# One column chunk of an output projection by seven half products, with another order of the jobs and loads around it

## The reference

```python
out = merge_heads(o_a, o_b, o_c) @ lp["w_o"]
xp = xp + g1 * mix
xp = xp + g2 * hier_moe(modulate(rms_norm(xp, lp["g_ffn"]), sh2, sc2), lp)
# in hier_moe: group logits and expert logits from h, top-1 group, top-2 experts in it, then
return (jax.nn.silu(xblk @ w1[e]) * (xblk @ w3[e])) @ w2[e]
```

## Time and profile before

| | |
|---|---|
| median of three runs | 1645.39 us (1644.51 to 1646.77) |
| the profiled execution | 1645.26 us, its span 1643.1 us |
| TensorE busy | 1532.1 us (93%) |
| weight loads of TensorE | 672.4 us (41%) |
| VectorE busy | 810.6 us (49%) |
| ScalarE, GpSimd busy | 281.4 us (17%), 101.3 us (6%) |
| the chain that ended last | TensorE 56%, DMA 29% of the span |
| matmuls of the projection (L1242) | 170.3 us, 384 records |

### The profile page before, as it was taken

How to read it: one execution, slowest core, us unless ns; L and a number is a source line. 1 busy time by engine, 2 the same in 40 slices (tenths; PEclk the granted TensorE clock), 3 DMA queues, 4 the chain that set the end, 5 groups by cost and what they waited for, 6 DMA issues and landing times.

```text
span 1643.1 us, 18272 instructions
## 1 busy us (share of the span) xinstructions
PE 1532.1 (93%) x6604; PEld 672.4 (41%) x6635; DVE 810.6 (49%) x1471; ACT 281.4 (17%) x746; POOL 101.3 (6%) x185
## 2 busy tenths in 40 slices
PE   6999999999999999999989889989989988988998
PEld 3446655454434444633333333333333333333332
DVE  3783555762365973525434434434434444434444
ACT  3124222122231000110210111111011012011010
POOL 1013100000131001000000000000000000000000
PEclk9999999999999999999999999999999999999999
DMA  9993521667597783999999999999999999999997
GB/s 391 418 413 150 198 110 73 251 247 307 182 391 314 307 326 135 329 399 407 428 428 428 429 428 427 429 427 426 425 428 426 426 427 425 426 428 425 424 424 285
DMA packets 62128, 581.96 MB, mean 354 GB/s; under 512 B 9218, under 2 KB 10178, under 8 KB 16940
## 3 DMA queue, kind: packets, MB, share of 16 engines
q1 hardware_dynamic: 54848, 557.34, 82.1%
q0 software_dynamic: 5936, 23.23, 3.6%
q10 hardware_dynamic: 1296, 0.77, 0.2%
HBM read 584.07 MB, written 7.05 MB: 360 GB/s over the span
## 4 chain that ended last, share of the span: by engine, by line
PE 56%; DMA 29%; DVE 2%; ACT 1%; issue 1%; SPq 1%; POOL 0%; DVEq 0%; ACTq 0%; POOLq 0%
DMA ring<-in_w 29%; PE bank L1539 13%; PE bank L1266 11%; PE bank L1242 9%; PE bank L1570 5%; PE bank L1437 5%; PE bank L1357 2%; PE bank L1488 2%; PE bank L1131 1%; PE bank L1332 1%; PE bank L1589 1%; DVE r L2112 1%; PE bank L1513 1%; PE bank L1340 1%; PE bank L1228 1%
## 5 line engine op out<-in xcount | busy, mean ns | idle before, releaser
L1539 PE MATMUL bank<-ring,r 128*64 128x512 f32 x1920 | 435.5, 601 | 36.8 <-DMA ring<-in_w 36.7
L1539 PEld LDWEIGHTS bank<-ring,r 128*64 128x64 f32 x1920 | 140.9, 138 | 304.5 <-issue 304.4
L1570 PE MATMUL bank<-ring,mod_row 128*64 128x512 f32 x896 | 208.3, 619 | 35.3 <-DMA ring<-in_w 27.4
L2370 DVE TENSOR_TENSOR bank<-bank,r 128x512 f32<-128x512 f32 x180 | 125.1, 695 | 210.6 <-PE bank L1437 210.5
L1266 PE MATMUL bank<-ring,r 128*128 128x384 f32 (+2 forms) x672 | 225.5, 494 | 0.0
L1242 PE MATMUL bank<-ring,r 128*128 128x512 f32 x384 | 170.3, 595 | 0.0
L1266 PEld LDWEIGHTS bank<-ring,r 128*128 128x128 f32 x672 | 123.6, 190 | 91.4 <-issue 43.7
L1570 PEld LDWEIGHTS bank<-ring,mod_row 128*64 128x64 f32 x896 | 77.0, 142 | 157.0 <-issue 146.9
L2372 DVE TENSOR_TENSOR r<-r,bank 128x512 f32<-128x512 f32 x180 | 123.8, 688 | 6.2
L1437 PE MATMUL bank<-r 128*128 128x512 bf16 x509 | 120.1, 380 | 4.9 <-issue 4.9
L2395 DVE TENSOR_SCALAR gains<-bank,w_now 128x512 f32<-128x512 f32 x30 | 22.5, 751 | 184.2 <-PE bank L1570 174.6
(11 more groups left out here) (302 smaller groups left out, 1282.4 us busy)
## 6 DMA issues: line engine op xcount, KB each, us to landing
ring<-in_w SPq DMA_DIRECT2D x174, 2048.0 KB, 17.3
ring<-in_w_mod SPq DMA_DIRECT2D x48, 1024.0 KB, 14.8
ring<-in_w SPq DMA_DIRECT2D x28, 1024.0 KB, 13.0
ring<-in_w_scale SPq DMA_DIRECT2D x16, 1024.0 KB, 21.7
ring<-in_w_shift SPq DMA_DIRECT2D x16, 1024.0 KB, 20.5
ring<-in_w_low SPq DMA_DIRECT2D x16, 1024.0 KB, 7.6
ring<-in_w_o SPq DMA_DIRECT2D x16, 1024.0 KB, 6.5
r<-mod_d POOLq DMA_DIRECT2D x8, 1024.0 KB, 7.6
```

What stands on the lines that cost most here:

```text
L1539: mm = pe.matmul(ps[64 * c:64 * c + 64, :], xg_t[:, j, 64 * c:64 * c + 64], big_cut(slot_of(u), (8, 512))[:, j % 8, :], start=(j == 0), st ...
L1570: mm = pe.matmul(y_ps[c][64 * h:64 * h + 64, :], act_t[:, f, 64 * h:64 * h + 64], big_cut(slot_of(u), (2, D))[:, c % 2, f * 512:(f + 1) * ...
L2370: v.tensor_tensor(ps[:, :], ps[:, :], g2b[:, min(t, 1), cols], ALU.mult).then_inc(strip_scaled, 1)
```

## The change

Chunk 2 of tiles 0 and 1 is one product of a 256x2048 by a 2048x512 matrix. It is cut in halves in each of the three dimensions (tile 0 and 1, rows 0 to 1023 and 1024 to 2047, columns 0 to 255 and 256 to 511), and done by seven half products with sums before and after (Strassen's scheme in Winograd's form) instead of eight. A half product is eight matmuls of 256 columns. VectorE makes the sums of the operands, 128x1024 a piece, into three ring places that `("hold", i)` units keep free, and joins the products, one of which ScalarE copies aside. The job order becomes (2,2), (2,0), (2,1), (3,0), (3,1), (3,2) behind job 5, so jobs 7 and 8 are the seven products (`SEVEN_AT` is 7) and the last weights' release moves from job 10 to job 8. The turns and logits of jobs 7 and 8 stand in and behind job 9; in job 11 the turn stands behind the first block and the logits of job 10 behind the second; the rank matmuls are spread accordingly. VectorE's normalised tiles follow jobs 9 and 10, and `choose(1)` and `first_slots(1)` move. `RING_FROM` is 10, and in the list of expert units the blocks 5 to 8 stand ahead of 11 and 4.

```diff
-OUT_ORDER = [(0, 0), (0, 1), (0, 2), (1, 0), (1, 1), (1, 2), (2, 0), (2, 1), (3, 0), (3, 1), (2, 2), (3, 2)]
+OUT_ORDER = [(0, 0), (0, 1), (0, 2), (1, 0), (1, 1), (1, 2), (2, 2), (2, 0), (2, 1), (3, 0), (3, 1), (3, 2)]
+SEVEN = 2
+SEVEN_AT = OUT_ORDER.index((SEVEN, 0))
+HELD = 3
-RING_FROM = 1
+RING_FROM = 10
...
+            if cc == SEVEN:
+                units.extend([("hold", i) for i in range(HELD)])
             units.extend([("out", cc, i) for i in range(4)])
...
+                    if s[1] == SEVEN:
+                        for i in range(HELD):
+                            frees[unit_no[("hold", i)]] = (acc_full, acc_uses)
...
                 if m >= SLOTS:
                     sp.wait_ge(*frees[m - SLOTS])
+                if u[0] == "hold":
+                    continue
...
-            for u in (17, *range(4), 11, 4, *range(5, 9), 12, 9, 10, 18, 19, 13, 14, 15, 20, 21, 16, 22, 23):
+            for u in (17, *range(4), *range(5, 9), 11, 4, 12, 9, 10, 18, 19, 13, 14, 15, 20, 21, 16, 22, 23):
...
+            def seven_products(n):
...
+                product(two, left, qo[:, 0, 0:8, :], part(0, left), start=True)
+                pe.wait_ge(sums_ready, 1)
+                product(two, right, x_first, w_first, stop=True)[-1].then_inc(product_done, 1)
+                turn_cols(n - 1)
+                pe.wait_ge(sums_ready, 2)
+                product(both, left, x_second, w_second, start=True)[-1].then_inc(product_done, 1)
+                product(one, left, qo[:, 0, 8:16, :], part(1, left), start=True)
+                pe.wait_ge(sums_ready, 3)
+                product(one, right, x_first, part(1, right), stop=True)[-1].then_inc(acc_full, 1)
+                pe.wait_ge(sums_ready, 5)
+                product(both, right, x_second, w_first, stop=True)[-1].then_inc(product_done, 1)
+                logits(n - 1)
+                pe.wait_ge(first_kept, KEPT_FROM + 1)
+                pe.wait_ge(sums_ready, 6)
+                mms = product(two, left, qo[:, 1, 8:16, :], w_second, start=True, stop=True)
+                for i in range(3):
+                    mms[i].then_inc(slot_free[ring_slot(us[i])], 1)
+                mms[-1].then_inc(acc_full, 1)
+                pe.wait_ge(sums_ready, 7)
...
+            def first_sums():
...
+                weight_sum(0, part(0, 1), part(0, 0))
+                v.tensor_tensor(x_first, x21, x22, ALU.add).then_inc(sums_ready, 1)
...
-                v.wait_ge(xa_ready, (9, 10, 12)[t])
+                v.wait_ge(xa_ready, (10, 11, 12)[t])
...
                     if n == len(OUT_ORDER) - 1:
                         first_slots(0)
-                        first_slots(1)
+                        choose(1)
                         squares_of_three()
+                    elif n == SEVEN_AT - 1:
+                        first_sums()
+                    elif n == SEVEN_AT:
+                        later_sums(n)
+                    elif n == SEVEN_AT + 1:
+                        last_join(n)
                     residual(n)
+                    if n == SEVEN_AT - 1:
+                        second_sums()
...
-                    elif n == 8:
+                    elif n == 9:
                         normalised(0)
-                    elif n == 9:
+                    elif n == 10:
                         choose(0)
                         normalised(1)
...
             last_factor()
+            first_slots(1)
             normalised_part(0, 2)
```

More of the change, by code:

```diff
@@ L359, in plan @@
     for n, (cc, t) in enumerate(OUT_ORDER):
-        if t == 0 and cc:
+        if cc and all(c != cc for c, _ in OUT_ORDER[:n]):
+            if cc == SEVEN:
+                units.extend([("hold", i) for i in range(HELD)])
             units.extend([("out", cc, i) for i in range(4)])
@@ L895, in moe_free, with hold @@
             return big_free[slot], m * each + rank
+        held = [unit_no[("hold", i)] for i in range(HELD)]
         def full_of(m):
-            return slot_full[ring_slot(m)], (m // SLOTS + 1) * 16
+            return slot_full[ring_slot(m)], 16 * sum(k not in held for k in range(m % SLOTS, m + 1, SLOTS))
+        def hold(i, shape):
+            slot = ring_slot(held[i])
+            return ring[:, slot, :].rearrange("p (a b) -> p a b", a=shape[0])
+        kept = cst[:, lay["mask"][0]:lay["mask"][0] + 512]
         def done_of(m):
@@ L1245, in out_part, with part, product @@
                     mm.then_inc(acc_full, 1)
-                elif t == TILES - 1:
+                elif t == TILES - 1 and cc != SEVEN:
                     mm.then_inc(slot_free[ring_slot(m)], 1)
+            def seven_products(n):
+                one, two, both = (acc[acc_of(n_turn + n + i)] for i in range(3))
+                left, right = slice(0, 256), slice(256, 512)
+                us = [unit_no[("out", SEVEN, i)] for i in range(4)]
+                acc_wait(n_turn + n + 1)
+                for m in us:
+                    arrived(m)
+                x_first, x_second = hold(2, (16, P))[:, 0:8, :], hold(2, (16, P))[:, 8:16, :]
+                w_first, w_second = (lambda k: hold(0, (8, 256))[:, k, :]), (lambda k: hold(1, (8, 256))[:, k, :])
+                def part(half, cols):
+                    return lambda k: cut(ring_slot(us[2 * half + k // 4]), (4, 512))[:, k % 4, cols]
+                def product(ps, cols, x, w, start=False, stop=False):
+                    return [pe.matmul(ps[:, cols], x[:, k, :], w(k), start=(start and k == 0), stop=(stop and k == 7))
+                            for k in range(8)]
+                product(two, left, qo[:, 0, 0:8, :], part(0, left), start=True)
[17 more added lines that the diff above has]
+                pe.wait_ge(sums_ready, 7)
             a = 0
@@ L1389, in _ @@
                         fold_g2()
-                    if no:
+                    if no == SEVEN_AT + 2:
+                        logits(no - 2)
+                    if no and no not in (SEVEN_AT, SEVEN_AT + 1, last_no):
                         logits(no - 1)
                     a += 1
-            last_no = len(OUT_ORDER) - 1
             pe.wait_ge(first_at, 1)
@@ L1998, in residual, with out_weights, weight_sum, own_sum @@
                 v.tensor_tensor(xs, ps[:, :], xs, ALU.add).then_inc(x1_ready, 1)
+            def out_weights(i, side):
+                u = ring[:, ring_slot(unit_no[("out", SEVEN, i)]), :].rearrange("p (j n) -> p j n", j=4)
+                return u[:, :, 256 * side:256 * side + 256]
+            def weight_sum(at, first, second):
+                for i in range(2):
+                    v.tensor_tensor(hold(at, (8, 256))[:, 4 * i:4 * i + 4, :], first(i), second(i), ALU.subtract)
+            def own_sum(at):
+                return lambda i: hold(at, (8, 256))[:, 4 * i:4 * i + 4, :]
@@ new lines, in part @@
+            def part(half, side):
+                return lambda i: out_weights(2 * half + i, side)
+            x11, x12, x21, x22 = qo[:, 0, 0:8, :], qo[:, 0, 8:16, :], qo[:, 1, 0:8, :], qo[:, 1, 8:16, :]
+            x_first, x_second = hold(2, (16, P))[:, 0:8, :], hold(2, (16, P))[:, 8:16, :]
+            def first_sums():
+                for i in range(4):
+                    v.wait_ge(*full_of(unit_no[("out", SEVEN, i)]))
+                for m in held:
+                    v.wait_ge(*frees[m - SLOTS])
+                weight_sum(0, part(0, 1), part(0, 0))
+                v.tensor_tensor(x_first, x21, x22, ALU.add).then_inc(sums_ready, 1)
@@ new lines, in second_sums, with later_sums @@
+            def second_sums():
+                v.wait_ge(sums_ready, 1)
+                v.tensor_tensor(x_second, x_first, x11, ALU.subtract)
+                for i in range(2):
+                    last = v.tensor_tensor(own_sum(1)(i), part(1, 1)(i), own_sum(0)(i), ALU.subtract)
+                last.then_inc(sums_ready, 1)
+            def later_sums(n):
+                one, both = acc[acc_of(n_turn + n)], acc[acc_of(n_turn + n + 2)]
+                v.wait_ge(product_done, KEPT_FROM + 1)
+                v.wait_ge(sums_ready, 2)
+                v.tensor_tensor(x_first, x12, x_second, ALU.subtract).then_inc(sums_ready, 1)
+                for i in range(2):
+                    last = v.tensor_tensor(own_sum(0)(i), part(1, 1)(i), part(0, 1)(i), ALU.subtract)
+                last.then_inc(sums_ready, 1)
+                v.wait_ge(product_done, KEPT_FROM + 2)
+                v.wait_ge(sums_ready, 3)
+                v.tensor_tensor(x_second, x11, x21, ALU.subtract).then_inc(sums_ready, 1)
+                for i in range(2):
+                    last = v.tensor_tensor(own_sum(1)(i), part(1, 0)(i), own_sum(1)(i), ALU.subtract)
+                last.then_inc(sums_ready, 1)
+                v.wait_ge(first_kept, KEPT_FROM + 1)
+                v.wait_ge(acc_full, n_turn + n + 1)
+                after(v.tensor_tensor(one[:, 0:256], one[:, 0:256], kept[:, 0:256], ALU.add))
+                v.wait_ge(product_done, KEPT_FROM + 3)
```

(12 more changed lines are left out.)

48 lines of the change are left out of this document (30 added, 18 removed).

## The result

The changed kernel takes 1647.53 us (median of 22 runs, 1645.23 to 1650.39); the kernel before, beside it, 1644.3 us (median of 22, 1641.6 to 1647.77). The ratio is 1.002, with a 95% interval of 1.0014 to 1.0026: 3.2 us slower, inside the bound of 0.2% that the prediction took for "no change". The profiled execution took 1648.44 us, beside 1645.26 us before; both lie about 1 us above their medians, so their difference can be read.

A forecast was written before the change was run, and what follows sets the result against it. TensorE bounds the output projection, the expert-weight stream everything behind about 797 us. The later of TensorE's +2.6 us (4.2 - 0.4 - 3.2 + 1.4 + 0.6) and DMA's +2.2, on 1645.26, gives 1647.9 us; range 1644.0 to 1651.5.

The forecast's parts named there:

- no change: Whole kernel: a difference under 0.2% (3.3 us) is about what a measurement can't tell from none.
- the likeliest case: Whole kernel: time within 0.2% of the kernel before, chance 0.54.
- first block waits for job 5's end: Job 6: the chunk's first load waits for job 5's last matmul, so TensorE starts 4.2 us later.
- wait of the fold: fold_g2's 0.36 us wait on VectorE's g2 steps vanishes behind the late start of job 6: minus 0.4 us.
- lower clock behind the gap: After TensorE's pause at job 6: half speed for about 3 us, a loss of 1.4 us (0 to 1.7).
- seven products for eight: Jobs 7 and 8: 112 records at 217 ns instead of 64 at 429, a gain of 3.2 us (2.4 to 3.4).
- VectorE's sums: Around the products: twelve added 128x1024 operations of about 1.2 us each, costing nothing.
- tail: Around the last output matmuls: moved logits and rank matmuls, shortening not earned back, a loss of 0.6 us (0 to 0.8).
- sum on TensorE: TensorE up to the expert stage: 4.2 - 0.4 - 3.2 + 1.4 + 0.6 = +2.6 us.
- The DMA queue: Expert loads: backlog of some 2.9 us, less 0.7 free at 735 to 740, gives +2.2 us (0.4 to 6.5).
- third rival: DMA queue, 680 to 705 us: backlog not made up, +4 to +6.5, at 1651; decided over 3.3 us; chance 0.30.
- the last place where the queue has room: Load stream at 735 to 740 us: the queue last runs dry there, DMA busy 0.86, 0.7 us free.

The follow-up runs named there:

- e8: Second run of e1's kernel, the changed kernel with held ring places listed behind chunk 2's four weight blocks: 1641.37 us, ratio to before 0.9986.
- e2: Changed kernel plus four matmuls of 128x512 with overwritten result ahead of job 6's first block, load untouched: 1645.27 us, ratio to before 1.0009.
- e7: Changed kernel plus two matmuls of 128x512 with overwritten result ahead of job 6's first block: 1646.81 us in a single run.
- e5: Changed kernel with jobs 7 and 8 as plain jobs of 32 matmuls, without products, sums and joins: 1652.46 us, ratio to before 1.0047.
- e3: Changed kernel with the load that waits for the second normalised tile put behind two other expert loads: 1646.85 us, ratio to before 1.0015.
- e4: Changed kernel plus two unused matmuls of 128x512 between the last gathering and the first expert matmul: 1649.79 us, ratio to before 1.0035.
- e1: Changed kernel with the held ring places listed behind chunk 2's four weight blocks instead of ahead: 1640.37 us, ratio to before 0.9978.

## Why the prediction came out as it did

It came out close: 1647.9 forecast, 1647.53 measured, within 0.2% of before, as the likeliest case said. The terms, from job 5's logits on:

| term | forecast | measured | from |
|---|---|---|---|
| first block waits for job 5's end | +4.2 | +4.15 | after, idle at job 6 |
| wait of the fold | -0.4 | -0.36 |, gone in after, back in e8 |
| lower clock behind the gap | +1.4 (0 to 1.7) | +3.0 | e2, e7 |
| seven products for eight | -3.2 | -3.29 | e5 |
| VectorE's sums | 0 | 0 | no idle time in L1285 |
| tail | +0.6 | +0.6 | below |
| sum on TensorE | +2.6 | +4.1 (4.17 in the table) | |

- **The gap** stood where the order of SyncE put it. It ended when one block alone had landed, 4.73 us after its issue at 589.91.
- **The products** took 24.2 us: 32 records of 256 columns took 7.07 us and 16 took 3.62, so 16 more cost 3.45, 216 ns a record, where 217 was taken. The sums took 1.2 us a piece, as the three nearest rows had it.
- **The tail.** From the start of job 7 to the end of job 11's matmuls after needs 72.35 us (615.08 to 687.43 in the chain below) and before 75.05 (608.66 to 683.71), 2.7 us less where the products alone save 3.3: so 0.6 was lost there. Behind it both need 13.4 us to the experts, though the logits of job 10 no longer stand there: the last turn waits for VectorE's residual until 689.01, 1.6 us behind the last matmul. The account of the prediction holds, though its own terms, 0.8 less 0.3, give 0.5 and not 0.6.

The chain of after that ended last, from job 7 on (start us, us, what; answers to the earlier trace rows):

```profile
615.08 6.99 PE bank L1285 x32
...
680.47 6.96 PE bank L1263 x16
...
689.01 0.75 PE bank L1189 x4
...
700.84 10.45 PE bank L1558 x48
```

- **The clock is the step that failed**, as a size. The prediction took half speed for about 3 us, from the loop's 3.5-us stretch behind a 2.7-us gap, with 1.7 as an upper bound. In the loop that bound is right: behind its pauses of 2.0 to 2.8 us either nothing was lost or 1.4 to 1.7 us (8.5 to 8.8 us where 32 records else take 7.09). Behind 4.15 us of idle time the lower clock held for 6.8 us, twice as long, and cost 3.0. The Trainium skill ("TensorE: Matmul & The Clock Gate", section "Why this matters for your kernels") warns of pauses between bursts; the trace agrees with its direction, and it was the rows from a shorter gap that made me put too little on it.
- **The DMA queue failed as a mechanism.** A backlog of 2.9 us was forecast (its own terms, 2.3 - 0.6 + 1.4, give 3.1). Of the 6.1 us that it says can be made up it counts 4.4, and no run shows the 1.7 us between them; what the runs show is 395 GB/s from 680 to 705 us of after where before moved 320, and a larger backlog all the same: the load that was issued at 697.35 landed 11.7 us later, at 709.1, 5.7 us behind its counterpart of before (issued 693.63, landed 703.4). By the third rival's own condition (over 3.3 us) the end should have moved by the queue. It did not. The step that fails is that 735 to 740 us is the last place where the queue has room. The trace of before shows another one, 33 us later. This is the busy share of its DMA engines from 772 to 785 us in 40 slices, each digit in tenths, and then that of after:

```profile
DMA  9980193146999897989989979999999999989999
```

```profile
DMA  9989989898999952993909795989799999989797
```

From 773.0 to 774.9 us the engines of before stand idle for some 1.4 us in sum, twice the 0.7 us at 735 to 740; after has such holes from 776.6 to 778.8, some 1.0 us in sum.

Three loads of 2048 KB of after, by the issue view (KB each, us to landing), issued at 723.31, 740.23 and 776.43:

```profile
ring<-in_w SPq DMA_DIRECT2D x1, 2048.0 KB, 17.8
...
ring<-in_w SPq DMA_DIRECT2D x1, 2048.0 KB, 9.2
...
ring<-in_w SPq DMA_DIRECT2D x1, 2048.0 KB, 7.5
```

Their counterparts of before were issued at 719.61, 736.51 and 772.72 and took 16.0, 7.4 and 8.4 us. So the landings are 5.5, 5.5 and 2.8 us later than before, the issues 3.7 each: the queue is 1.8 us behind TensorE up to 749 us, and no longer at 784, where a load issued on TensorE's release takes what the one at 736.51 took in a dry queue. From there the stream starts from TensorE's releases, which is what e3 and e4 say by their ends.

**Why it came out close all the same.** It did so in part by luck. TensorE's loss was 1.6 us more than forecast. Against it, the stage behind E took 0.5 us less than in the profile of before and A came 0.47 us earlier, which no term foresaw; and the forecast was counted from the profiled execution of before, 1645.26 us, which lay 1.0 us above the median of 22. So the forecast difference was 2.6 us and the measured one 3.2. What shortens the last stage by 0.2 to 0.7 us in all nine others stays open.

## What to carry to other kernels

Seven products for eight pay here exactly what the columns say, but the places that they borrow must be taken from the ring where nothing in front of them is needed soon: the same units listed four places later turned a loss of 3 us into a gain of 3. A wait on the bounding engine is to be priced with what its clock does behind it, and for that a gap of the same length is wanted, not a shorter one. Before a queue's backlog is held against a change, follow landings against issues until a load finds the queue dry: only what is left there counts.

## What the runs showed of the hardware

- Half clock for 6.8 us behind a 4.15-us pause of TensorE (3.0 us lost), 9.31, 9.88 and 10.17 us for the same 16 records in e3, e5 and e4 with pauses of 4.19, 4.30 and 4.21 us, where 7.11 is undisturbed: the price varied between 2.2 and 3.1 us, and not with the length of the pause.
- The clock can fall early in the kernel too, without a pause of that size. TensorE's largest idle time around 211 us is 0.91 us in e1, and 0.92 in after, where the clock stayed full; the clock in that stretch of e1's profiled execution, and then of after's:

```profile
209.00:219.00 10.00, 9.09 (x18) 3.96 (x17) 5.85 (x15) 3.58 (x10) 1.04 (x2) 0.66 0.01 2
```

```profile
209.00:219.00 10.00, 9.08 (x28) 4.67 (x27) 7.21 (x16) 3.51 (x10) 1.01 (x2) 1.00 0.00 1
```

  It put all that followed 3.4 us late (A at 593.00, in after 589.65), and it has nothing to do with the edit: the same kernel in e8 did not have it, and of the other profiled executions only e5's did (0.66). A single profiled execution is not a kernel's time.
- A load of 1024 KB that is alone in the queue landed 4.7 us after its issue; with others ahead of it, the next blocks landed 2.5 us apart (594.64, 597.11 and 599.60 us in after). What the first block of a burst costs is its latency, not its share of the rate.
